# Expert stage: h2 is made again from the x1 rows that the last norm loads, instead of stored and loaded; expert lists for two tiles

## The reference, cut to what matters

```python
x1 = layer_norm(ALPHA * x + gate1 * mix, ln1_g, ln1_b)
h2 = x1 * (1 + scale2) + shift2
# for each token: 8 heads, product keys, 16 best of 16384 experts for each head
q  = h2 @ w_pq ; s = q . sub_keys ; e, cv = top 16 of the sums of two top-16 lists
g  = softmax(cv) ; a = gelu(peer_u[e] . h2) ; f = sum over e of g * a * peer_v[e]
y  = layer_norm(ALPHA * x1 + gate2 * f, ln2_g, ln2_b)
```

## Time and profile before

| | |
|---|---|
| median of 3 runs | 3920.98 us (3920.7 to 3922.79) |
| the profiled execution: its time, its span | 3916.33 us, 3914.5 us |
| expert stage, first dot product to last instruction | 1125.2 to 3914.5 us |
| busy: PE, DVE, ACT, POOL | 3263.4, 2498.0, 1226.2, 1504.2 us |
| gathers of 1 MB | 1056 |
| HBM read, written | 1335.42 MB, 28.83 MB |

### The profile page before, as it was taken

How to read it: one execution, slowest core, us unless ns; L and a number is a source line. 1 busy time by engine, 2 the same in 40 slices (tenths; PEclk the granted TensorE clock), 3 DMA queues, 4 the chain that set the end, 5 groups by cost and what they waited for, 6 DMA issues and landing times.

```text
span 3914.5 us, 42745 instructions
## 1 busy us (share of the span) xinstructions
PE 3263.4 (83%) x12854; PEld 1547.8 (40%) x12854; DVE 2498.0 (64%) x6184; ACT 1226.2 (31%) x3479; POOL 1504.2 (38%) x1312
## 2 busy tenths in 40 slices
PE   7799988888789978878878878888778888888976
PEld 6444656666334333333333333333333333333322
DVE  2111246566388847777777777776676677768975
ACT  2110025555124322332333333232332233323332
POOL 0000003555223334444445445445444444444343
PEclk9899999999899989999999999999999999999999
DMA  9502137899769999999999999999999999999997
GB/s 380 199 35 48 48 122 256 294 310 322 260 273 362 387 413 417 420 420 417 417 418 406 419 419 406 419 412 413 416 410 410 414 418 413 413 412 407 418 413 309
DMA packets 280415, 1366.99 MB, mean 349 GB/s; under 512 B 38450, under 2 KB 59779, under 8 KB 142977
## 3 DMA queue, kind: packets, MB, share of 16 engines
q0 software_dynamic: 171648, 1170.53, 74.0%
q1 hardware_dynamic: 77788, 157.64, 11.2%
q10 hardware_dynamic: 30756, 36.20, 2.7%
HBM read 1335.42 MB, written 28.83 MB: 349 GB/s over the span
## 4 chain that ended last, share of the span: by engine, by line
DMA 38%; PE 18%; DVE 9%; issue 3%; ACT 2%; POOL 2%; ACTq 0%; DVEq 0%; SPq 0%; POOLq 0%
DMA sb_early<-in_uv,sb_experts 30%; PE psum L1605 14%; DMA sb_late<-in_uv,sb_experts 8%; DVE sb_early L1902 4%; PE psum L1591 2%; POOL sb_early L1532 2%; PE psum L1561 2%; DVE sb_late L1902 1%; ACT sb_diag L1702 1%; ACT sb_expert_w L1694 1%; POOL sb_late L1532 1%; ACT sb_gelu L1691 0%; DVE sb_si L1810 0%; DVE sb_ci L1810 0%; DVE sb_bn L1777 0%
## 5 line engine op out<-in xcount | busy, mean ns | idle before, releaser
L1605 PE MATMUL psum<-sb_early,sb_diag 128*128 128x512 f32 x3376 | 1594.4, 618 | 385.8 <-ACT sb_diag L1702 385.6
L1532 POOL DMA_INDIRECT sb_early<-in_uv,sb_experts x844 | 1015.4, 1203 | 1197.8 <-PE psum L1605 1050.9
L1902 DVE CUSTOM_DVE_ANT_0 sb_early<-sb_early,sb_h 128x1024 f32<-128x1024 f32 x844 | 1029.1, 1226 | 534.0 <-DMA sb_early<-in_uv,sb_experts 502.5
L1605 PEld LDWEIGHTS psum<-sb_early,sb_diag 128*128 128x128 f32 x3376 | 635.4, 195 | 1320.3 <-issue 682.1
L1691 ACT ACTIVATE sb_gelu<-sb_dots 128x2 f32<-128x2 f32 x528 | 107.3, 203 | 1798.2 <-DVE sb_dots L1902 1797.5
L1605 PE MATMUL psum<-sb_late,sb_diag 128*128 128x512 f32 x848 | 405.2, 622 | 110.4 <-ACT sb_diag L1702 110.3
L1532 POOL DMA_INDIRECT sb_late<-in_uv,sb_experts x212 | 253.1, 1194 | 400.2 <-PE psum L1605 288.4
L921 POOL DMA_INDIRECT sb_v_pages<-in_cache_v,sb_v_row_of x240 | 229.6, 957 | 431.1 <-PE psum L948 207.1
L1702 ACT ACTIVATE sb_diag<-sb_ident,sb_expert_w 128x128 f32<-128x128 f32 x1024 | 355.2, 394 | 16.7
L1902 DVE CUSTOM_DVE_ANT_0 sb_late<-sb_late,sb_h 128x1024 f32<-128x1024 f32 x212 | 258.5, 1226 | 135.6 <-DMA sb_late<-in_uv,sb_experts 128.7
L1605 PEld LDWEIGHTS psum<-sb_late,sb_diag 128*128 128x128 f32 x848 | 160.7, 197 | 349.6 <-ACT sb_diag L1702 176.1
(11 more groups left out here) (251 smaller groups left out, 3090.2 us busy)
## 6 DMA issues: line engine op xcount, KB each, us to landing
sb_low<-in_cache_k SPq DMA_DIRECT2D x256, 256.0 KB, 3.0
sb_w_ada<-in_w_ada SPq DMA_DIRECT2D x12, 2048.0 KB
sb_early<-in_uv,sb_experts POOLq DMA_INDIRECT x844, 17.1
sb_w_pq<-in_w_pq ACTq DMA_DIRECT2D x4, 2048.0 KB, 27.1
merged_scratch<-sb_merged ACTq DMA_DIRECT2D x8, 1024.0 KB
sb_early<-merged_scratch SPq DMA_DIRECT2D x8, 1024.0 KB, 20.8
sb_w_bcu<-in_w_in SPq DMA_DIRECT2D x12, 512.0 KB, 7.0
sb_rows<-x_scratch SPq DMA_DIRECT2D x9, 512.0 KB, 7.8
```

The costliest lines, as they stand in the source:

```text
L1532: pool.indirect_dma_start(ring(n), None, uv, bass.IndirectOffsetOnAxis(ap=e_all[:, t, k + s:k + s + 1], axis=0))\
L1605: ins = nc.tensor.matmul(psum[:, 2 * (t % 2) + n, :], diag[:, q % CHAINS, s, :], ring(q * PAIR + s)[:, D + n * BANK:D + (n + 1) * BANK], s ...
L1902: nc.vector.tensor_tensor_reduce(u, u, h[:, t % 2, :], 1.0, 0.0, ALU.mult, ALU.add, dots[:, q % CHAINS, s:s + 1]).then_inc(T["dots_ready"], 1)
```

## The change

- Prompt tiles 1 to 7: h2 is no longer stored and loaded. `mix_hidden` runs for tiles 0 and 8 alone. `residual(t)` now loads x1 of tile t much sooner, into one of two buffers, and DVE makes h2 from it (`hidden_made`, at the pair that the new table `DVE_MADE` gives: 45, 83, 140, 201, 265, 329, 393 for tiles 1 to 7). The same buffer later serves `finish(t, 1)`. `residual(t + 2)` is issued when `finish(t, 1)` has run.
- Tile 8: h2 is made in `mix_hidden`, stored in four copies, and loaded once the dots of tile 6 are done; x1 is stored and loaded as 32 rows once, not as four copies.
- gate2 of the sample tile is loaded once (32 rows) after the last dots of tile 7, into the h2 buffer that is free by then, not in four copies with the other constants.
- `sc2` and `sh2` of the prompt get a buffer of their own; the expert lists and gates keep two tiles, not nine (`e_all`, `g_all`).
- For tile 1 the turn, its copy and the first scores come one pair later (46, 47, and 48 and 49).
- SP's order changes with it.

```diff
-            PE_SCORES.setdefault(first - 3 + part // 2 if b == 4 else first - 10 + part, []).append((b, part))
+            PE_SCORES.setdefault(first - 2 + part // 2 if b == 4 else first - 10 + part, []).append((b, part))
         if b % 4 == 0:
-            PE_TURN.setdefault(first - 5 if b == 4 else first - 20, []).append(b // 4)
-            ACT_TURN.setdefault(first - 4 if b == 4 else first - 14, []).append(b // 4)
+            PE_TURN.setdefault(first - 4 if b == 4 else first - 20, []).append(b // 4)
+            ACT_TURN.setdefault(first - 3 if b == 4 else first - 14, []).append(b // 4)
+            if b // 4 < TILES:
+                DVE_MADE[first - 5 if b == 4 else first - 22] = b // 4
...
-        lng, gate2, x_res, f = rows[:, 0:2], rows[:, 2:4], rows[:, 4], rows[:, 5]
+        sc2, sh2 = modulated[:, 0], modulated[:, 1]
+        lng, gate2, x_res, f = rows[:, 0:2], rows[:, 2], rows[:, 3:5], rows[:, 5]
...
                 def residual(t):
-                    sp.dma_start(x_res, x1_t[:, t, :]).then_inc(T["xres_land"], 16)
+                    n = rows_of(t)
+                    src = x1_dram[SEQ:SEQ + NS, :] if t == TILES else x1_t[:, t, :]
+                    sp.dma_start(x_res[0:n, t % 2], src).then_inc(xres_land[t % 2], 16)
...
                     x1_store(t)
-                    if t:
-                        h2_store(t)
...
-                hidden(1)
                 for u in range(3):
                     sp.wait_ge(x_stored[u], X1_TOTAL[u])
-                    sp.wait_ge(h_stored[u], H2_TOTAL[u])
+                residual(1)
+                sp.wait_ge(T["h2_ready"], 2)
+                for g in range(COPIES):
+                    sp.dma_start(h2_dram[SEQ + g * NS:SEQ + (g + 1) * NS, :], x_in[0:NS]).then_inc(T["h2_stored"], 16)
...
                 for t in range(TILES + 1):
+                    if t == TILES - 2:
+                        sp.wait_ge(T["dots_ready"], (t + 1) * SEL)
+                        sp.dma_start(h[:, 0], h2_dram[SEQ:SEQ + P, :]).then_inc(T["h2_land"], 16)
+                    if t == TILES - 1:
+                        sp.wait_ge(T["dots_ready"], (t + 1) * SEL)
+                        sp.dma_start(h[0:NS, 1], row(GATE2)[1:NC, :].unsqueeze(1).to_broadcast([NB, NT, D])).then_inc(T["gate_land"], 16)
                     if t + 2 <= TILES:
-                        sp.wait_ge(T["dots_ready"], (t + 1) * SEL)
-                        hidden(t + 2)
-                    if t < TILES:
                         sp.wait_ge(T["xres_free"], t + 1)
-                        residual(t + 1)
+                        residual(t + 2)
...
+                def hidden_made(t):
+                    dve.wait_ge(xres_land[t % 2], 16 * (t // 2 + 1))
+                    step(nc.vector.tensor_tensor(h[:, t % 2], x_res[:, t % 2], sc2, ALU.mult))
+                    step.done()
+                    step(nc.vector.tensor_tensor(h[:, t % 2], h[:, t % 2], sh2, ALU.add))
+                    step.tell(T["h2_made"])
...
                 mix_norm(1)
-                mix_hidden(1)
...
                     if q in M_NORM:
                         mix_norm(M_NORM[q])
-                    if q in M_HIDDEN:
-                        mix_hidden(M_HIDDEN[q])
+                        if M_NORM[q] == TILES:
+                            mix_hidden(TILES)
+                    if q in DVE_MADE:
+                        hidden_made(DVE_MADE[q])
```

More of the change, by code:

```diff
@@ L1319, in opened @@
         return 1 + SPACING * (t - BEFORE)
-    DVE_PIECES, ACT_EXP, DVE_GATES, PE_TURN, ACT_TURN, PE_SCORES = ({} for _ in range(6))
+    DVE_PIECES, ACT_EXP, DVE_GATES, PE_TURN, ACT_TURN, PE_SCORES, DVE_MADE = ({} for _ in range(7))
     for g in range(READY, HEADS + PH):
@@ L1360, in experts @@
         oT = sbuf(st, "oT", [P, H, P])
-        e_all = sbuf(st, "experts", [P, TILES + 1, SEL], U32)
-        g_all = sbuf(st, "gates", [P, TILES + 1, SEL])
+        e_all = sbuf(st, "experts", [P, 2, SEL], U32)
+        g_all = sbuf(st, "gates", [P, 2, SEL])
         fold = sbuf(st, "fold", [P, P])
@@ L1404, in experts @@
         m_land, m_back = sem("pr_m_land"), sem("pr_m_back")
[L1405 to L1406 removed]
+        x_land, x_stored = ([sem(f"pr_{n}{u}") for u in range(3)] for n in ("x_land", "x_stored"))
+        xres_land = [sem(f"pr_xres_land{u}") for u in range(2)]
         dve_c, act_c = sem("pr_dve"), sem("pr_act")
[L1408 removed]
         x1_t = x1_dram.rearrange("(t p) d -> p t d", p=P)
@@ L1414, in experts @@
         COPIES = P // NS
-        X1_TOTAL = [16 * sum((COPIES if t == TILES else 1) for t in range(TILES + 1) if t % 3 == u) for u in range(3)]
-        H2_TOTAL = [16 * sum((COPIES if t == TILES else 1) for t in range(1, TILES + 1) if t % 3 == u) for u in range(3)]
+        X1_TOTAL = [16 * sum(1 for t in range(TILES + 1) if t % 3 == u) for u in range(3)]
         def at(q):
@@ L1447, in x1_store @@
                     sp.wait_ge(T["x1_ready"], t + 1)
-                    if t < TILES:
[L1449 to L1463, removed]
+                    dst = x1_dram[SEQ:SEQ + NS, :] if t == TILES else x1_t[:, t, :]
+                    sp.dma_start(dst, x_of(t)[0:rows_of(t)]).then_inc(x_stored[t % 3], 16)
                 def residual(t):
-                    sp.dma_start(x_res, x1_t[:, t, :]).then_inc(T["xres_land"], 16)
+                    n = rows_of(t)
+                    src = x1_dram[SEQ:SEQ + NS, :] if t == TILES else x1_t[:, t, :]
+                    sp.dma_start(x_res[0:n, t % 2], src).then_inc(xres_land[t % 2], 16)
                 sp.dma_start(sub[:], A["subln_w"].to_broadcast([P, DV])).then_inc(T["small"], 16)
@@ L1763, in mix_evict @@
                     n = rows_of(t)
-                    new, x = h2_of(t)[0:n], x_of(t)[0:n]
+                    new, x = gated_of(t)[0:n], x_of(t)[0:n]
                     if t == TILES:
                         dve.wait_ge(T["rows2_land"], 48)
-                        step(nc.vector.tensor_scalar(sc2[0:NS], sc2[0:NS], 1.0, None, ALU.add))
+                        step(nc.vector.tensor_scalar(sc2_s[0:NS], sc2_s[0:NS], 1.0, None, ALU.add))
                     dve.wait_ge(T["mix_psum"], t + 1)
@@ L1869, in piece @@
                         k = (j % 2 if t == TILES else j) * TOPK
-                        step(nc.vector.scalar_tensor_tensor(out=e_all[rows, t, k:k + TOPK], in0=eab[rows, 0], scalar=float(PK),
+                        step(nc.vector.scalar_tensor_tensor(out=e_all[rows, t % 2, k:k + TOPK], in0=eab[rows, 0], scalar=float(PK),
                                                             in1=eab[rows, 1], op0=ALU.mult, op1=ALU.add))
@@ L1889, in gates @@
                     k = 0 if t == TILES else j * TOPK
-                    dst = g_all[rows, t, k:k + 2 * TOPK].rearrange("p (h k) -> p h k", k=TOPK)
+                    dst = g_all[rows, t % 2, k:k + 2 * TOPK].rearrange("p (h k) -> p h k", k=TOPK)
                     step(nc.vector.tensor_tensor(dst, cv[rows, s], over(gsum[rows, s], TOPK), ALU.mult))
@@ L1910, in finish @@
                         else:
-                            dve.wait_ge(T["consts2"], 16 * (3 + COPIES))
+                            dve.wait_ge(T["consts2"], 48)
+                            dve.wait_ge(T["h2_stored"], 16 * COPIES)
+                        if t == TILES:
+                            dve.wait_ge(T["gate_land"], 16)
                         sums = flat(psum[:, 2 * (t % 2):2 * (t % 2) + 2, :])
-                        step(nc.vector.tensor_tensor(f, sums, gate2[:, t // TILES], ALU.mult))
+                        step(nc.vector.tensor_tensor(f, sums, h[:, 1] if t == TILES else gate2, ALU.mult))
                         step.tell(T["f_free"])
                     elif n == 1:
-                        dve.wait_ge(T["xres_land"], 16 * (t + 1))
-                        step(nc.vector.scalar_tensor_tensor(out=f, in0=x_res, scalar=ALPHA, in1=f, op0=ALU.mult, op1=ALU.add))
+                        dve.wait_ge(xres_land[t % 2], 16 * (t // 2 + 1))
+                        step(nc.vector.scalar_tensor_tensor(out=f, in0=x_res[:, t % 2], scalar=ALPHA, in1=f, op0=ALU.mult, op1=ALU.add))
                         step.tell(T["xres_free"])
```

39 lines of the change are left out of this document (19 added, 20 removed).

## The result

| | before | changed |
|---|---|---|
| median of 4 runs | 3921.89 us (3920.7 to 3928.82) | 3894.26 us (3891.8 to 3900.22) |
| ratio | | 0.9925, 95% interval 0.9909 to 0.9941 |
| five more runs, beside 13 of before | 3918.62 us (3909.02 to 3932.1) | 3895.87 us (3894.06 to 3903.47) |
| ratio | | 0.9946, 95% interval 0.9933 to 0.996 |
| the profiled execution: its time, its span | 3916.33, 3914.5 us | 3893.64, 3891.8 us |

The change makes the kernel faster, by 0.5 to 0.8%: 27.6 us between the first medians, 22.8 between the second, 22.7 between the two profiled executions. Forecast were 18.2 us and 3902.8 us, with 3897 as the low end. The sign was right; the first median lies 2.7 us under the range, the second 1.1.

What follows compares the result with a forecast made beforehand. DVE, then PE, then from 1340 us the gathers' transfer rate bound the expert stage. Savings of 13.2 us (transfers) and 5.0 us (earlier start) sum to 18.2, taking 3921.0 to 3902.8 us; range 3897 to 3911.

Steps and rivals of the forecast that it cites:

- part 1: Where DMA is full, from about 1340 us: removed transfers, 10.25 units of 512 KB at 1.29 us, save 13.2 us.
- What bounds the stage: Expert stage: DVE limits 1130 to 1155 us, PE to 1340 us, the gathers' transfer rate from there on.
- the upper bound: In part 1, gate2's three copies cost 1.0 us beyond their bytes, which makes that term 14.2 us.
- Part 2: Before 1155 us, where DVE limits: removing mix_hidden of tiles 1 and 2 starts everything behind it 5.0 us sooner.
- Part 3: 1155 to 1340 us: mix_hidden of tiles 3 to 7 removed, DVE's 12 us hidden by PE, gain nothing.
- Parts 4 and 5: With DMA full, hidden_made's 2.5 us of DVE per tile and 3.9 us x1 waits at tiles 4 to 7 cost nothing.
- the cover: Gathers standing in line before the DMA engines hide delays of DVE up to 17.2 − 5.9 = 11.3 us.
- the sign that I named against the forecast: DMA's share falling under 1.00 at the waits for x1 and scores would show the forecast wrong.
- Part 6: Tile 1's scores come one pair later; DVE, asking at 1448.84 us, waits 8.3 us once, at no cost.
- rival C: hidden_made and its waits on DVE hold back gathers until DMA runs dry: slower, 3944 us, chance 0.05.

Runs made afterwards that it cites:

- e5: Changed kernel with mix_hidden of tiles 1 to 7 done by DVE again, results unused: 3901.9 us in one run, stage 1.1 us over e4.
- e6: Changed kernel with seven more 512 KB stores of x1, tiles 1 to 7: 3896.09 us in one run, stage 0 to 1.1 us more.
- e2: Changed kernel with 24 more 512 KB loads, four at each of tiles 2 to 7: ratio 1.0024, 1.26 us each.
- e11: Changed kernel with 20 more 512 KB stores where DMA is full: 3921.9 us in one run, 1.23 us each.
- e10: Changed kernel with the sample tile's x1 stored in four copies and loaded as 128 rows again: 3896.62 us in one run, first to last dot 1.7 us more.
- e7: Changed kernel with 16 more gate2 loads of 32 rows, 128 KB each: 3915.03 us in one run, 0.94 us each.
- e13: Kernel before with only gate2's load changed, one of 32 rows behind tile 7's last dots: 3915.89 us in one run, first to last dot 2770.5 us.
- e4: Changed kernel with mix_hidden of tiles 1 and 2 done by DVE again, result unused: ratio 0.9963, stage 4 to 5.2 us more.
- e3: Changed kernel with hidden_made of tiles 2 to 7 and the transposes behind it three pairs later: ratio 0.9945, first to last dot 1.5 us longer.
- e8: Changed kernel with ten more 1.25 us DVE operations in each hidden_made, tiles 1 to 7: 3961.45 us in one run, stage 62.5 us more.

## Why the prediction was right, and where it missed

The step that failed is in part 1: the copies of gate2 were priced by their bytes, 1.0 us for three, and cost about 3. The second miss is the range, whose low end had no room for the scatter of runs: the stage's 22.5 us taken from the 3921.0 of before would have been 3898.5, inside it.

- *What bounds the stage*: right. Stores and DVE work before 1340 us cost 0 to 1.1 us in each of e5 and e6, transfers behind it 1.23 to 1.26 us for 512 KB (e2, e11); 1.29 was taken.
- *Part 1, the transfers*: this is the term that was mis-sized. Taken were 13.2 us. Measured: seven loads at 1.26 make 8.8, x1's copies and rows 1.7 (e10; 1.9 taken), tile 7's store at most 1.1 (e6), and gate2's three copies 2.8 to 3 (e7, e13) where 1.0 was taken and 2.0 was the upper bound. Together 13.3 to 14.6. The prices of the others came out a little under what was taken, so the whole is off by less than its worst term. The sign was in the profile: the 10 us about those copies moved 362 GB/s, and I set it aside as a bound. Even the bound was too low: the dip and the bytes together make 2.6 us for four, and e13 shows 4. That window holds nearly the whole dip. Here is the rate of the kernel before from 1360 to 1450 us, in slices of 2.25 us, where it is the 379, 313 and 302; so what is missing can't be read from the rate.

```profile
GB/s 422 426 411 430 422 426 430 422 430 426 422 421 411 428 428 437 406 419 410 422 428 419 411 415 410 422 379 313 302 415 431 415 415 419 426 422 411 408 415 422
```

- *Part 2, the start*: 5.0 us predicted; 6.2 and 5.3 in the two traces of the changed kernel (first row to pair 4), 4 to 5.2 with the work put back (e4). Right.
- *Part 3*: costed at nothing, and e5's 1.1 us are within the scatter of traces. Right.
- *Parts 4 and 5, the bumps*: that they cost nothing was right (e3), and the wait came as worked out, 3.5 to 4.2 for 3.9. The reason was a little too generous: the cover is 8.2 to 11.5 us and 9.5 in the mean, not 11.3 (e8). I had taken the shortest landing, 5.9 us, from a stretch where one gather goes after another; into a line just emptied it takes 9.1. With 6.9 us of bump the margin was 1.3 at the least, not 4.4. And the sign that I named against the forecast, DMA under 1.00, came without the loss.
- *Part 6*: 7.07 us of wait for 8.3. From pair 40 to 64 the changed kernel takes 133.5 and 134.2 us where e13, with this wait not yet made, takes 134.4 and still has the copies of x1. About 1 us of it at most can have been lost.
- *The sum.* The measured terms make 14.0 in the middle for part 1 and 4.6 for part 2: 18.6 of the 22.5 us by the stage, 19.7 with e5's 1.1 for part 3. About 3 to 4 us stay unassigned, of which two traces of one kernel differ by 1.1. By stretch, 1.1 of them (the mean of the traces) lie in the start and 1.3 from pair 64 to 448, where the traces of before scatter by 1.6.
- *The range* was too narrow at its low end. It was built from terms alone, with no room for the scatter of runs, though the profiled execution of before stood 4.65 us under its median. The first measurement is 27.6 us, of which the stage explains 22.5. That the mechanism was right and the time still fell outside is due to both: 2 us of gate2 and the rest of the unassigned gain in the stage, 5 us between the medians outside it.
- The Trainium skill's rule on the shared port ("SBUF — State Buffer", "SBUF: two separate sides") was weighed into rival C. No run here separates it: in e8, with seventy more such operations on DVE, nothing of the loss needs it, and nothing rules it out.

## What to carry to other kernels

Where gathers stand in line, a plain transfer of whole tiles costs its bytes at the full rate, load or store, and is free only where something else is the limit: look up each transfer's place before pricing it. Where a dip in the rate stands beside a transfer of another form, price that form by itself, with an experiment. Gaps in the packet rate are not yet lost time; look whether the consumer waits longer. To cost a change of half a percent, compare stages within traces from a fixed instruction on, and give the range of the whole program's time the scatter of its runs.

## What the runs showed of the hardware that I hadn't expected

- A load of 128 KB that broadcasts 8 rows of HBM to 32 partitions cost 0.94 us among gathers, a plain 512 KB load 1.26, and six units of 128 KB of plain rows 1.7 together. While such loads ran the packets of the gathers took longer too, 2.70 us of the 16 engines' time for 1 MB where it is 2.42 (e7).
- DMA's packets may cover only half of the engines' time for 8 us (share 0.48) while landings go on every 2.5 us. By the estimate above, a gather's packets were over 8 us before its landing. What holds the landing back isn't shown by these traces.
- Ten gathers of 1 MB in a ring, landing in 17.2 us at the median, cover a pause of 8.2 to 11.5 us in their consumer (six places in e8), about half of the landing time.
